# Gathering expert 1's columns inside expert 0, with a narrower gather ahead of the first expert and 31 filler matmuls at the start

## The reference, cut to what matters

```python
h = layer_norm(DEEPNORM_ALPHA * h + mix, ln1_g, ln1_b)
logits = (t @ router_w + router_b)
top_v, top_i = lax.top_k(logits, 4)          # 4 of 32 experts for each token
gates = jax.nn.softmax(top_v, axis=-1)
# for each expert e, over the rows `tok` routed to it:
hid = clamped_swiglu(t[tok] @ w_gate[e] + b_gate[e], t[tok] @ w_up[e] + b_up[e])
out[tok] += gate[tok, None] * (hid @ w_down[e] + b_down[e])
h = layer_norm(DEEPNORM_ALPHA * h + out, ln2_g, ln2_b)
```

## Time and profile before

| | |
|---|---|
| median of 3 runs | 1058.4 us (1058.15 to 1058.66) |
| the profiled execution | 1057.99 us, its span from first to last instruction 1056.2 us |
| PE busy | 1019.8 us of the span, 97% |
| DVE, ACT, POOL busy | 228.7, 143.8, 30.6 us |
| DMA | 426.21 MB, mean 404 GB/s |
| GB/s in the first ten of 40 slices (26.4 us each) | 314 274 412 191 267 314 357 432 426 436 |
| GB/s in the slices after | 426 to 434 nearly throughout, 419 and 238 in the last two |
| chain that ended last | PE 69%, DMA 29%, ACT 1% |

### The profile page before, as it was taken

The page is one execution under the profiler, slowest core; times in us unless marked ns, Lnnn a source line. Parts: engine busy times, 40 slices in busy tenths (PEclk is TensorE's granted clock), DMA queues, the critical chain, the costliest instruction groups (busy, mean ns, idle before and its releaser), DMA issues.

```text
span 1056.2 us, 12142 instructions
## 1 busy us (share of the span) xinstructions
PE 1019.8 (97%) x5116; PEld 448.6 (42%) x5116; DVE 228.7 (22%) x495; ACT 143.8 (14%) x348; POOL 30.6 (3%) x50
## 2 busy tenths in 40 slices
PE   8999999999999999999999999999999999999997
PEld 7888764333333333332333333333333333233332
DVE  5453652111111111111111112211111111111112
ACT  3312331111111111101110011111111111011102
POOL 1230100000000000000000000000000000000000
PEclk9999999999999999999999999999999999999999
DMA  9894889999999999999999999999999999999995
GB/s 314 274 412 191 267 314 357 432 426 436 431 429 430 433 432 431 431 434 432 431 431 434 431 429 430 431 433 430 431 428 434 432 432 429 434 426 426 428 419 238
DMA packets 40587, 426.21 MB, mean 404 GB/s; under 512 B 6986, under 2 KB 19411, under 8 KB 24036
## 3 DMA queue, kind: packets, MB, share of 16 engines
q1 hardware_dynamic: 38516, 424.12, 95.9%
q10 hardware_dynamic: 2032, 1.53, 0.6%
HBM read 424.59 MB, written 1.05 MB: 403 GB/s over the span
## 4 chain that ended last, share of the span: by engine, by line
PE 69%; DMA 29%; ACT 1%; DVE 0%; issue 0%; SPq 0%; POOL 0%; DVEq 0%; POOLq 0%; ACTq 0%
PE bank L1215 29%; DMA ring<-in_moe_w_up 18%; PE bank L1266 15%; DMA ring<-in_moe_w_gate 11%; PE bank L1195 4%; PE bank L1187 4%; PE bank L871 3%; PE bank L886 2%; PE bank L1061 2%; PE bank L1049 1%; PE bank L1003 1%; PE bank L1257 1%; PE bank L1135 1%; PE bank L964 1%; PE bank L1069 1%; PE bank L1235 1%
## 5 line engine op out<-in xcount | busy, mean ns | idle before, releaser
L1215 PE MATMUL bank<-ring,arena 128*64 128x512 f32 x1980 | 444.5, 601 | 24.5 <-DMA ring<-in_moe_w_up 20.7
L1215 PEld LDWEIGHTS bank<-ring,arena 128*64 128x64 f32 x1980 | 141.3, 138 | 297.3 <-issue 253.6
L1266 PE MATMUL bank<-ring,arena 128*64 128x512 f32 x1024 | 226.8, 595 | 1.5 <-issue 1.5
L1266 PEld LDWEIGHTS bank<-ring,arena 128*64 128x64 f32 x1024 | 71.5, 137 | 151.7 <-issue 150.1
L1663 DVE COPY arena<-bank 128x512 f32<-128x512 f32 x32 | 22.1, 692 | 326.1 <-PE bank L1266 326.1
L756 ACT ACTIVATE arena<-arena 128x512 f32<-128x512 f32 x32 | 20.1, 630 | 451.4 <-DVE arena L1650 451.4
L1195 PE MATMUL bank<-arena 64*128 64x512 f32 x256 | 72.0, 640 | 0.9 <-DVE arena L1663 0.9
L1187 PEld LDWEIGHTS bank<-arena 128*128 128x128 f32 x480 | 58.8, 196 | 22.8 <-issue 22.8
L1657 DVE TENSOR_SCALAR arena<-bank 128x512 f32<-128x512 f32 x32 | 22.1, 692 | 209.2 <-PE bank L1215 209.2
L767 ACT ACTIVATE arena<-bank 128x512 f32<-128x512 f32 x32 | 19.1, 597 | 336.3 <-PE bank L1257 336.3
L1187 PE MATMUL bank<-arena 128*128 128x128 f32 x480 | 64.5, 288 | 0.0
(11 more groups left out here) (281 smaller groups left out, 514.6 us busy)
## 6 DMA issues: line engine op xcount, KB each, us to landing
ring<-in_moe_w_down SPq DMA_DIRECT2D x25, 4096.0 KB, 28.3
ring<-in_moe_w_gate SPq DMA_DIRECT2D x24, 4096.0 KB, 24.7
ring<-in_moe_w_up SPq DMA_DIRECT2D x24, 4096.0 KB, 27.5
ring<-in_moe_w_down SPq DMA_DIRECT2D x10, 2048.0 KB, 16.6
ring<-in_moe_w_gate SPq DMA_DIRECT2D x9, 2048.0 KB, 21.4
ring<-in_moe_w_up SPq DMA_DIRECT2D x9, 2048.0 KB, 15.1
ring<-in_w_in SPq DMA_DIRECT2D x12, 1024.0 KB, 11.9
ring<-in_moe_w_gate SPq DMA_DIRECT2D x8, 1024.0 KB, 17.9
```

Of the source, the lines that this page charges most:

```text
L1215: ins = mm(b[h * SL:(h + 1) * SL, :], (xA[pp], xB)[q][:, k, par * SL:(par + 1) * SL], columns(unit_at(m, kt), h), start=False, stop=kt == ...
L1266: ins = mm(bank[6][h * SL:(h + 1) * SL, :], hidT[:, kt % 4, (kt // 4) * SL:(kt // 4 + 1) * SL], unit_at(2, kt)[:, h * 512:(h + 1) * 512], ...
```

## The change

1. `keep_clock` at the start of PE's program issues 31 matmuls instead of 18.
2. The gather ahead of expert 0 uses the first 64 columns of `sel` alone, expert 0's, and the copies behind it are 64 columns wide.
3. Expert 1's columns are gathered inside expert 0 by a new function, `gather_second`: half 0 (8 matmuls of 64 columns, bank 7) where the pair gather stood, half 1 (bank 5) in two parts, 4 matmuls behind the transposes of the hidden rows and 4 behind the down projection. ACT copies both with a new function, `second_expert_evac`, and counts `xT_ok` once, behind the second half.
4. Experts 2 and 3 are gathered inside expert 1, both halves: half 0 where a gather stood before, half 1 (bank 5) between the transposes and the scatter. DVE makes their one-hot ahead of expert 1 instead of ahead of expert 0. From expert 2 on all is as before.

```diff
@@ scalar
-            def xT_evac(g, half, b, dst, done, upto=4):
+            def xT_evac(g, half, b, dst, done, upto=4, width=2 * SL, both=False):
...
-                    ins = nc.scalar.activation(dst[:, k, :], b[:, k * P:(k + 1) * P], ACT.Identity, bias=bq[:, half, k:k + 1],
+                    ins = nc.scalar.activation(dst[:, k, 0:width], b[:, k * P:k * P + width], ACT.Identity, bias=bq[:, half, k:k + 1],
                                                scale=gq[:, half, k:k + 1])
+                if done is None or half or not both:
+                    ins.then_inc(xT_ok, 1)
+
+            def second_expert_evac():
+                for half, dst, b in ((0, xA[0], bank[7]), (1, xB, bank[5])):
+                    act.wait_ge(second_gath_ps, NT + half + 1)
+                    for k in range(4):
+                        ins = nc.scalar.activation(dst[:, k, SL:2 * SL], b[:, k * SL:(k + 1) * SL], ACT.Identity, bias=bq[:, half, k:k + 1],
+                                                   scale=gq[:, half, k:k + 1])
                 ins.then_inc(xT_ok, 1)
...
-                if ahead is not None:
+                if first:
+                    second_expert_evac()
+                elif second:
+                    xT_evac(n + 1, 0, bank[7], xA[ahead], n + 1, both=True)
+                    xT_evac(n + 2, 1, bank[5], xB, n + 1)
+                elif ahead is not None:
                     xT_evac(n + 2, par, bank[7], xB if par else xA[ahead], n + 1)
@@ tensor
-            keep_clock(bank[1], 18)
+            keep_clock(bank[1], 31)
...
-                    ins = mm(banks[k][:, k * P:(k + 1) * P], row_group(h1p[:, t, :], 4 * half + k, 4), sel[:, t, :],
+                    ins = mm(banks[k][:, k * P:k * P + SL], row_group(h1p[:, t, :], 4 * half + k, 4), sel[:, t, 0:SL],
...
+            def gather_second(b, half, groups):
+
+                for k in groups:
+                    for t in range(NT):
+                        ins = mm(b[:, k * SL:(k + 1) * SL], row_group(h1p[:, t, :], 4 * half + k, 4), sel[:, t, SL:2 * SL],
+                                 start=t == 0, stop=t == 1)
+                return ins
...
                 if first:
                     pe.wait_ge(GT_ok, 1)
-                if gathers is not None:
+                    gather_second(bank[7], 0, range(4)).then_inc(second_gath_ps, 1)
+                elif gathers is not None:
                     gather(*gathers, bank[7])
...
                 ins.then_inc(hidT_ps, 1)
+                if first:
+                    gather_second(bank[5], 1, (0, 1))
+                if second:
+                    gather(gathers[0] + 1, gathers[1], 1, bank[5])
...
+                if first:
+                    gather_second(bank[5], 1, (2, 3)).then_inc(second_gath_ps, 1)
@@ vector
             for k in range(UNROLL):
-                tile(k, k % 2, k == 0, k + 1, k + 2 if k % 2 == 0 else None)
+                if k == 1:
+                    dve.wait_ge(second_gath_ps, 2 * NT)
+                    select(NT, 2, 2)
+                tile(k, k % 2, k == 0, k + 1, k + 2 if k == 2 else None)
```

More of the change, by code:

```diff
@@ L266, in build @@
         scat = [sem(f"scat{t}") for t in range(NT)]
+        second_gath_ps = pos_ps
         var2, rstd2, fin = sem("var2"), sem("rstd2"), sem("fin")
@@ L767, in tile @@
                 nc.scalar.activation(hidT[:, :, :].rearrange("p c n -> p (c n)"), bank[4][:, :], ACT.Copy).then_inc(hidT_ok, 1)
-                if ahead is not None:
+                if first:
[4 more added lines that the diff above has]
+                elif ahead is not None:
                     xT_evac(n + 2, par, bank[7], xB if par else xA[ahead], n + 1)
-            xT_evac(0, 0, bank[7], xA[0], None, 2)
-            xT_evac(1, 1, bank[6], xB, None)
+            xT_evac(0, 0, bank[7], xA[0], None, 2, SL)
+            xT_evac(1, 1, bank[6], xB, None, 4, SL)
             for k in range(UNROLL):
@@ L1239, in tile @@
                 last = isinstance(n, int) and n == NE - 1
+                second = isinstance(n, int) and n == 1
                 if last:
@@ L1318, in experts @@
                     tile(n, k % 2, first, unit_at, arrived, k // 2,
-                         (n + 2, it * (UNROLL // 2) + (k // 2 + 1), k % 2) if ahead else None, not first,
+                         (n + 2, it * (UNROLL // 2) + (k // 2 + 1), 0 if isinstance(n, int) and n == 1 else k % 2) if ahead else None, not first,
                          n - LATE if isinstance(n, int) and n in (LATE, LATE + 1) else None)
@@ L1597, in _ @@
             for k in (2, 3):
-                ins = ts(xA[0][:, k, :], bank[5][:, k * P:(k + 1) * P], gq[:, 0, k:k + 1], bq[:, 0, k:k + 1], ALU.mult, ALU.add)
+                ins = ts(xA[0][:, k, 0:SL], bank[5][:, k * P:k * P + SL], gq[:, 0, k:k + 1], bq[:, 0, k:k + 1], ALU.mult, ALU.add)
             ins.then_inc(xT_dve, 1)
```

## The result

The changed kernel takes **1070.34 us** (median of 4 runs, 1069.58 to 1071.55); the kernel before took 1058.28 us beside it (1057.93 to 1058.66). The ratio is 1.0112, 95% interval 1.0099 to 1.0124: 12.1 us slower, where the prediction had 4.8 and its range ended at 1065.3. The direction and, as it turns out, the 4.9 us of the queue were right; 7 us came from places that the prediction had written off.

A forecast was written before the change was run, and what follows sets the result against it. The prediction took the DMA queue moving expert weights as the bound: profiled 1057.99 us + 1.8 (start less copies) + 3.1 (queue dry) = 1062.9, in the median 1063.3; it predicted 1063.2 us, +0.45%, range 1060.1 to 1065.3.

The forecast's parts named there:

- the 4.9 us of the queue: How much later the DMA queue moves the same bytes: by the prediction's slacks 1.8 us at 190 us, 4.9 at 280.
- The queue as the bound: From about 190 us, 402 MB of expert weights pass at about 430 GB/s; the last dry moment sets the end.
- The dips: Stretches under 430 GB/s near 192, 213 and 243 us, where the queue runs dry for 0.6, 1.9 and 0.6 us.
- the 1.8 in the sum: Lateness of everything from expert 0 on: 1.9 us from the start less 0.1 from narrower copies.
- the slack "only grows": After expert 3's down projection (4.2 us of queued work), PE needs 26.5 us an expert, the queue 29.2.
- The fillers, +1.9: Start of PE's program: 26 more records take 2.90 us, 0.74 free, about 0.25 absorbed; all PE 1.9 us later from 12.10.
- The narrow gather saves nothing on PE: Ahead of expert 0: 64 columns for 128 leave the step near 0.12 us, set by weight loading; saving 0.
- the rival of the half step: Narrow gathers step at 0.06 us, saving 1.4 us on the first gather; 1060.5 us in all; chance 6%.
- Expert 1 starts 2.8 us later than expert 0 does: Behind expert 0's down projection, the last 4 gather matmuls (0.94 us) and ACT's copies (1.29 us) delay expert 1 by 2.8.
- Expert 1's own gather, +2.0: Inside expert 1, ahead of its down projection: 16 more gather records put PE another 2.0 us later, 4.8 in all.
- a tail that the change leaves alone: After the queue's last bytes, the kernel's end was taken to cost the same as before: 0 us more.
- The rival "the stall drops the clock": The wait ahead of expert 1 lowers PE's clock, 1.7 us more on PE; 1065.0 us in all; chance 12%.

## Why the prediction was wrong

*The queue as the bound: right up to 280 us.* The dips came where they were named, and the lateness of the queue in the changed kernel's profile is the predicted 4.9 us. That the two agree to 0.1 us is in part luck. The start gave 2.4 us for the 1.8 in the sum, and what the gathers added behind it was 2.5 for 3.1 (2.4 in the kernel with 18 fillers, where they stand alone): two errors of 0.6 us that cancel. That the slack "only grows" from expert 3 on does not hold, see the open points.

*The fillers, +1.9: right in kind, not a constant.* PE resumes at 12.03 instead of 9.41 and expert 0 is 2.42 late. In the kernel before with 31 fillers PE resumes at 10.98, and the queue loses 1.6 us by it; in the pair with the wide gather (18 and 31 fillers) it is 2.3 at 280 us. The sum took the slow records ahead of 7.33 us as given; how long they last changes with the execution.

*The narrow gather saves nothing on PE: right* (3.02 against 3.07 us), and the rival of the half step is dead. That it costs nothing is in doubt: with 18 fillers some executions take 3 to 4 us longer, and the profiles of such show the clock down from inside it.

*Expert 1 starts 2.8 us later than expert 0 does: right* (5.16 - 2.42 = 2.74). The gap is 1.38 us, and it goes when the second gather stands ahead of the down projection.

*Expert 1's own gather, +2.0: right* (2.05 us for the group; the issue goes from 5.16 late at 190.97 to 7.03 at 212.12).

*The step that failed: "a tail that the change leaves alone".* The tail's instructions are the same, but their place in PE's program is not, and 115 instructions more moved the target of the jump over the extra pass out of the fetched blocks. That is 3.3 us of branch, of which 2.8 are exposed, and 3.2 us of half clock behind it, 6.05 together. Adding 108 instructions to the kernel before brings the same end; adding 80 to the changed kernel takes it away. 4.9 + 0.4 (the drift of the last experts in this profile) + 6.05 are the 11.4 us between the two spans.

*The rival "the stall drops the clock": real, in some executions.* I gave it 12% as a case of its own, at 1065.0. It is no alternative to the forecast but an addition that comes in a part of the executions. It may be the source of the 0.7 us between the spans' difference of 11.4 and the medians' 12.1; the unprofiled executions can't be looked into, so that is not shown.

*Open, and a fourth cost that the traces do show.* Five profiles lose another 0.9 to 1.7 us of the queue between 600 and 800 us, where all kernels run the same code; the eight others lose at most 0.4. The five are those in which the clock is at its lower level in expert 15's up projection, just ahead of expert 16, whose w_gate and most of whose w_up lie outside the ring. Before, and in the kernel before with 108 instructions more:

```profile
581.24 7.09 PE L1215 MATMUL bank<-ring,arena 128*64 128x512 f32 x32 [0.86 <-DMA ring<-in_moe_w_up]
```

```profile
581.92 8.78 PE L1215 MATMUL bank<-ring,arena 128*64 128x512 f32 x32 [1.92 <-DMA ring<-in_moe_w_up]
```

Expert 16 then starts 2.4 us later (602.45 for 600.07), and the queue dips to 317 GB/s at 630 to 633 us. In the nine other profiles this projection takes 7.09 us. There the up projection of expert 14 takes 8.7 to 8.8, and behind it PE still waits 0.9 us for expert 15's w_up, so that the delay is taken up.

A second such place is expert 4's gate projection and the sums of the biases ahead of it (8 records of 32x512). In the best version below the projection takes 8.73 us instead of 7.04, and the lateness goes from 1.3 us at 260 to 1.7 at 280:

```profile
267.99 8.73 PE L1238 MATMUL bank<-ring,arena 128*64 128x512 f32 x32
```

All ten kernels with added small matmuls have a fall there, at 265 to 276 us, and the four without have none; all five with the step at 600 us are among the ten. The small matmuls run only near 990 us, so why they should matter is open. But the kernels that were shifted carry a cost that is not the change's. What part of the end's 6.05 us would be left without the fall of the clock was not measured apart.

No version beat the kernel before. The best, with the wide gather, 18 fillers, the second gather ahead of the down projection and the shift, is 1.0019 of it. Its queue is 0.8 us late from 180 us on, behind the down projection that starts 1.1 us late; expert 1's extra gather, near 243 us, and the fall at 268.3 bring this to 1.8.

## What to carry to other kernels

When a change adds or removes instructions ahead of a jump over a long block, count them: the price of the jump depends on where it and its target stand in the fetched blocks, and code that "the change leaves alone" can slow by 6 us in 1060. Look at the duration of the branch itself, at the packets of the instruction queue and at what PE waits for behind it, and put the jump where its target is fetched, with room behind the target. And before you narrow a matmul that is bound by its weight load, ask what it wins: here nothing on PE, and in three of eight profiles the clock fell inside it. Last, a time that is added at the start of a program can vary with the execution, and a shift that is meant to do nothing but move code needs a kernel of its own to be held against: here the shifted kernels all had a fall of the clock that the unshifted ones had not.

## What the runs showed of the hardware

- A jump 308 instructions ahead took 350 to 460 ns with its target in the block behind the current one, and 3.37 to 3.67 us with it one block further, or with that block's edge crossed only 8 instructions earlier. With the edge 76 instructions earlier it was cheap, and the trace has a packet 5.4 us ahead of the branch.
- A jump back finds more. The loop over experts 4 to 15 fetches four 16 KB packets from 270 to 375 us, in its first round, and none from 380 to 610 us, in the other two (the kernel before). So more than two blocks stay.
- Straight code just behind a jump also stalls where it runs into the next block: 1.94 us idle with the edge 4 instructions behind the target, 0.58 with 15.
- After 1.9 to 2.75 us of such a stall the clock was at its lower level for 6.8 us or more; after 0.58 us it was not. Two profiles had it at the lower level in the last group with no such stall ahead.
- An f32 gather matmul with 128 x 128 weights steps at about 0.12 us with 64 moving columns as with 128, and in 3 of 8 profiles the clock fell inside a run of 64-column ones.
- A wait of 1.38 us on PE was followed within about 1 us by the lower level in 3 of 6 profiles, in kernels that have the same code at this place.
- 62 records of 128x128 fillers at the start took 8.64 us in one profile and up to 9.94 in others.
